# Sums and lows of the up forms ahead of the next weight low on VectorE

## The reference

```
h = rmsnorm(x, g[NORM_PRE_MLP])
x = x + rmsnorm(jnp.square(jax.nn.relu(h @ mlp_w1[l])) @ mlp_w2[l], g[NORM_POST_MLP])
```

## Time and profile before

| | us |
|---|---|
| median of 3 runs | 1434.55 (1434.52 to 1434.6) |
| the profiled execution's own time | 1434.28 |
| its span in the trace | 1432.5 |
| PE busy | 1421.0 (99%) |
| DVE busy | 771.7 (54%) |
| ACT busy | 617.5 (43%) |
| granted TensorE clock, mean | 0.999 |
| the first up slab's relu | starts at 1109.01 in the trace |
| the first down product of the last segment | begins at about 1382 |

### The profile page before, as it was taken

The page is one execution under the profiler, slowest core; times in us unless marked ns, Lnnn a source line. Parts: engine busy times, 40 slices in busy tenths (PEclk is TensorE's granted clock), DMA queues, the critical chain, the costliest instruction groups (busy, mean ns, idle before and its releaser), DMA issues.

```text
span 1432.5 us, 17397 instructions
## 1 busy us (share of the span) xinstructions
PE 1421.0 (99%) x7066; PEld 1156.6 (81%) x7066; DVE 771.7 (54%) x1326; ACT 617.5 (43%) x1013; POOL 82.8 (6%) x69
## 2 busy tenths in 40 slices
PE   9999999999999999999999999999999999999998
PEld 8867778887888888886777788887779888888886
DVE  6577857855243364465355244573355645656545
ACT  4455541225234343355346324453343654535342
POOL 0000000022120001000000110000000101001000
PEclk9999999999999999999999999999999999999999
DMA  6210223222322244541110424253123995768511
GB/s 202 64 46 32 74 89 117 89 88 75 102 65 82 70 145 150 176 132 45 31 59 30 162 88 147 90 176 103 59 89 127 244 239 139 197 172 184 168 74 59
DMA packets 127938, 160.42 MB, mean 112 GB/s; under 512 B 7365, under 2 KB 98754, under 8 KB 127603
## 3 DMA queue, kind: packets, MB, share of 16 engines
q1 hardware_dynamic: 117088, 133.51, 29.0%
q0 software_dynamic: 10624, 25.73, 8.3%
q10 hardware_dynamic: 146, 0.07, 0.0%
HBM read 155.06 MB, written 4.24 MB: 111 GB/s over the span
## 4 chain that ended last, share of the span: by engine, by line
PE 98%; DVE 1%; ACT 1%; issue 0%; DMA 0%; DVEq 0%; ACTq 0%
PE dense L809 24%; PE dense L811 24%; PE dense L810 24%; PE score L955 4%; PE score L972 3%; PE turned L972 3%; PE turned L955 2%; PE turned L965 1%; PE score L965 1%; PE score L809 1%; PE score L811 1%; PE score L810 1%; PE turned L811 1%; PE turned L809 1%; PE turned L810 1%; PE score L1126 1%
## 5 line engine op out<-in xcount | busy, mean ns | idle before, releaser
L809 PE MATMUL dense<-hidden_high,weight_high 128*128 128x512 f32 (+1 forms) x840 | 327.1, 389 | 0.0
L811 PE MATMUL dense<-hidden_high,weight_low 128*128 128x512 f32 (+1 forms) x840 | 320.7, 382 | 0.0
L810 PE MATMUL dense<-hidden_low,weight_high 128*128 128x512 f32 (+1 forms) x840 | 320.4, 381 | 0.0
L1495 ACT ACTIVATE weight_high<-raw 128x1024 fp32r<-128x1024 f32 (+5 forms) x178 | 211.9, 1227 | 218.5 <-PE dense L811 194.0
L2014 DVE TENSOR_TENSOR weight_low<-raw,weight_high 128x2048 fp32r<-128x2048 f32 (+2 forms) x78 | 158.9, 2046 | 192.5 <-ACT weight_high L1495 192.4
L811 PEld LDWEIGHTS dense<-hidden_high,weight_low 128*128 128x128 f32 x840 | 157.9, 188 | 30.8
L810 PEld LDWEIGHTS dense<-hidden_low,weight_high 128*128 128x128 f32 x840 | 158.2, 188 | 29.2 <-issue 0.5
L809 PEld LDWEIGHTS dense<-hidden_high,weight_high 128*128 128x128 f32 x840 | 158.1, 188 | 29.0 <-issue 0.5
L2009 DVE TENSOR_TENSOR weight_low<-raw,weight_high 128x1024 fp32r<-128x1024 f32 (+1 forms) x98 | 104.3, 1113 | 91.6 <-ACT weight_high L1495 91.6
L809 PE MATMUL dense<-weight_high,hidden_high 128*128 128x256 f32 (+1 forms) x288 | 82.0, 285 | 0.1
L811 PE MATMUL dense<-weight_high,hidden_low 128*128 128x256 f32 (+1 forms) x288 | 81.2, 282 | 0.0
(11 more groups left out here) (379 smaller groups left out, 2501.0 us busy)
## 6 DMA issues: line engine op xcount, KB each, us to landing
raw<-in_w_in SPq DMA_DIRECT2D x33, 1024.0 KB, 5.3
raw<-in_mlp_w SPq DMA_DIRECT2D x23, 1024.0 KB, 5.6
raw<-in_w_branch SPq DMA_DIRECT2D x12, 1024.0 KB, 5.3
down_raw<-in_mlp_w SPq DMA_DIRECT2D x12, 1024.0 KB, 6.1
raw<-in_mlp_w POOLq DMA_DIRECT2D x9, 1024.0 KB, 8.6
raw<-in_nsa_cmp_w SPq DMA_DIRECT2D x8, 1024.0 KB, 5.4
raw<-in_cross_wkv SPq DMA_DIRECT2D x8, 1024.0 KB, 5.2
down_raw<-in_mlp_w POOLq DMA_DIRECT2D x6, 1024.0 KB, 12.1
```

The lines of the kernel that those rows point to most:

```text
L809: pe.matmul(out_ap, ah, bh, start=first, stop=False)
L810: pe.matmul(out_ap, ah, bl, start=False, stop=False)
L811: return pe.matmul(out_ap, al, bh, start=False, stop=last)
L1495: return nc.scalar.activation(dst, src, ACT.Copy, scale=scale)
```

## The change

VectorE's stream in segments 0 to 2: for the first three up slabs of each segment, the sums and the form lows of the slab now stand ahead of the weight low; for the fourth the order is as it was. No instruction is added or removed, and the streams of the other engines are the same.

```
             for g in range(SEGMENTS - 1):
                 for u in range(4 * g, 4 * g + 4):
-                    low(slab_at["up", u] + 2)
+                    if u % 4 == 3:
+                        low(slab_at["up", u] + 2)
                     up_sums(u)
                     up_low(u)
+                    if u % 4 != 3:
+                        low(slab_at["up", u] + 2)
                 for i in range(FORMS):
                     low(slab_at["form", g, i] + 2)
```

## The result

| | before | changed |
|---|---|---|
| median | 1434.55 us | 1441.91 us (1440.53 to 1443.77, 4 runs) |
| the profiled execution's own time | 1434.28 us | 1440.53 us |
| its span | 1432.5 us | 1438.7 us |
| ratio of the times | | 1.0052, 95% interval 1.0037 to 1.0068 |

The runs of the changed kernel are 3.2 us apart, those of before 0.1; of the 68 runs of the kernel before that were timed beside the experiments, 66 lie between 1434.0 and 1434.7, the other two at 1435.61 and 1436.46. The profiled execution happens to be the fastest of the four, so its rows show 6.25 us of the loss.

What follows compares the result with a forecast made beforehand. The prediction took TensorE, busy 1421.0 of 1432.5 us, to bound the kernel. A 4.66 us stall plus 1.3 of clock, 5.96 together, on 1434.55 gave 1440.5 us, range 1438.9 to 1443.0.

Steps and rivals of the forecast that it cites:

- The stall of slab 2: TensorE's first weight load of slab 2 waits for the low moved behind up slab 0's form lows: 4.66 us.
- The new slab timing of 7.33 us: On VectorE, a moved 128x2048 weight low ends 7.33 us after the start of its slab's square.
- The clock: The stall lowers TensorE's clock, so the matmuls behind it run slower: 1.3 us, with 0 and 1.9 for the range.
- the rival in which it stays up: At slab 2 the stall comes but TensorE's clock does not fall: 1439.2 us, chance 0.18.
- double that: Bracketed addition to the clock term's 1.9 us bound: doubled if the clock comes back only at a second look.
- Slab 1: Up slab 1, low of slab 3: done by 1126.8, needed by TensorE at 1130.0; no cost, 3.2 us of cover.
- Slabs 4, 5, 8 and 9: Their moved weight lows are ready 0.35 us before TensorE loads, at four places: no cost, little cover.
- Slabs 2, 6 and 10, and SyncE: Low of form (g, 0), line 2702's later transfer with 1.1 us before TensorE feels it, SyncE's later loads: no cost.
- the 12.6 of segment 0: Line 2702's transfer took 12.6 us in segment 0, put down to another ahead in the queue; later issue makes this less likely.
- the rival of further stalls: Cover fails at four slabs or three transfers: one late transfer gives 1443.3 us, three 1448.9; chance 0.14.
- ScalarE's waits: ScalarE's waits for VectorE's sums from 1100 us on fall from 17.9 us to about 9.

Runs made afterwards that it cites:

- The filled gap: The changed kernel with 18 idle matmuls on TensorE between slab 1 and slab 2: 1439.36 us (5 runs), ratio 1.0034 to the kernel before.

## Why the prediction was right, and where it was not

**The stall of slab 2** was right in place, cause and size. The new slab timing of 7.33 us from square to end of low was measured as 1119.00 - 1111.70 = 7.30. The stall was worked out as 4.66, and the trace shows 4.70 on the weight load. The filled gap, which leaves the clock out, costs 4.9 in the medians. Slab 0 alone gives 7.0 of the 7.4 us.

**The clock** fell as forecast, and the rival in which it stays up is out: no run of the changed kernel is below 1440.5, and none has a mean clock above 0.998. The term was sized at 1.3 us and measured 2.5 in the median (filled against unfilled), 1.6 and 2.9 in the two profiles: this is the term of the sum that was too small. Two readings behind it were off. The fall was put at 2.3 us after the last matmul, by one row of the program's end; in the three profiles with the stall of 4.5 us it came 3.1, 3.8 and 4.5 us after that matmul's end, so less of the low state fell into the stall, where it costs nothing. And I took 3.8 us, all that the span's end shows, for the length of the low state, though that stretch is cut off by the end of the program: it was 3.4 us in two profiles and 6.8 in two. So the upper bound of 1.9 was too low as well. Without the bracketed "double that", for which no row of the kernel before stood, the range would have ended at 1441.1 and missed the 1441.9; that part was luck.

**Slab 1** was right in the changed kernel and would have misled anyone who put slab 0 back: its 3.2 us of cover existed only behind a stall of 4.66. Moved alone it costs 1.4 us.

**Slabs 4, 5, 8 and 9** kept their cover of 0.35 us, in the changed kernel and alone.

**Slabs 2, 6 and 10, and SyncE.** The transfer for form (g, 2) was the right thing to look at, and its landing (8.4, 8.7 and 9.1 us in the three segments, so the 12.6 of segment 0 is gone, as argued) came within the cover as worked out. What I missed is the next one in the same queue, for form (g, 4). The prediction asked only whether line 2700's late transfer holds back line 2702, and it does not; but line 2704, which waits for its landing, it does hold back. In the changed kernel the transfer for form (1, 4) is issued at 1227.24, 4.8 us late after the stall and the clock are taken off, and takes 13.0 us instead of 10.1. Of 9 us of cover that leaves 1.2. It costs nothing in most runs; in the two profiles in which it used up the cover, with seven and with nine slabs moved, TensorE lost 1.6 us. This was the rival of further stalls in miniature, by another transfer than the one named. How much of it is in the changed kernel's median is not settled: its two profiles and that of slab 0 alone show no such wait, and the medians differ by 0.4 us.

**ScalarE's waits** fell to 9.3 us, as forecast (about 9), and TensorE gained nothing from it.

## What to carry to other kernels

When one engine is busy 99% of the span, look for the moment at which it asks for the result that the change delays; the share of other engines' waits that goes away says nothing. Check the first turn of a pipelined loop by itself, since its spacing can be half of the steady one: here the weights of slab 2 were due 5.4 us after the relu of slab 0, those of slab 6 10.5 us after the relu of slab 4 (1185.83 to 1196.28). And when a stall is taken away, work out every cover behind it again: it may have been the stall that gave it.

## What the runs showed of the hardware

- A wait of TensorE of 4.5 us lowered its clock to 1.2 GHz in each of the three profiled executions that had it, and one of 2.1 us did in one; by their mean clocks (0.997 or 0.998, against 0.999 or 1.000), in all fourteen runs with the first and in five of seven with the second. A wait of 1.3 us left the clock at 1.00 in the two profiles that have it.
- The low stretch was 3.4 or 6.8 us long and began 2.6 to 4.5 us after the end of the last matmul before the wait, so it costs 1.6 to 2.9 us beyond the wait. It also moves the runs apart: the changed kernel's nine runs span 3.2 us. Not all spread is the clock's, since with slabs 0 or 0 and 1 put back the runs spread by 3.3 and 2.2 us at mean clocks of 0.999 and 1.000.
- 18 idle matmuls in the gap kept the clock at 1.00 and gave back 2.5 us, although the kernel still waited for the same low.
- A 1 MB transfer that adds to what is in SBUF took 8.3 to 8.8 us in the kernel before when little else moved (1207.40, 1212.24, 1238.91), and 12.5 and 13.2 us beside SyncE's loads with no other adding transfer under way (1169.44, 1250.54). The one for form (g, 4) took 10.1 to 12.0 us before and 13.0 to 15.9 in the changed kernel's first two segments, 12.3 and 13.9 in its third. What of that is the other adding transfer, issued 0.8 to 3.0 us ahead, and what SyncE's loads is not separated.
